# Memory attention in high and low parts, token-major values, and reordered evictions in a two-layer decoder trunk

## The chip, the cores and the metric

The kernel runs on one core of one Trainium2 chip. The metric is the device time of one execution in microseconds. Times in a profile are counted from the first instruction of the span.

## The reference

1024 tokens of width 1024 go through two layers. Each layer is: RMSNorm, one input projection, sparse attention (index scores, the 256 highest keys of a query, 8 heads) beside differential attention (4 heads), output projection and residual; RMSNorm and cross-attention into 256 memory tokens; RMSNorm and a gated MLP of width 2816 with a convolution of width 3. The part at which most of the change works:

```python
def _memory_attention(xn, memn, w_q, w_kv, w_o):
    b, s, _ = xn.shape
    m = memn.shape[1]
    q = (xn @ w_q).reshape(b, s, MEM_HEADS, MEM_HEAD_DIM)
    k, v = jnp.split(memn @ w_kv, 2, axis=-1)
    k = k.reshape(b, m, MEM_HEADS, MEM_HEAD_DIM)
    v = v.reshape(b, m, MEM_HEADS, MEM_HEAD_DIM)
    logits = jnp.einsum('bqhd,bkhd->bhqk', q, k,
                        preferred_element_type=jnp.float32) * MEM_HEAD_DIM ** -0.5
    p = jax.nn.softmax(logits, axis=-1)
    o = jnp.einsum('bhqk,bkhd->bqhd', p.astype(v.dtype), v).reshape(b, s, D_MODEL)
    return o @ w_o
```

There are 4 memory heads of 256 dimensions. The RMSNorm ahead of w_q is xn = h * rsqrt(mean(h*h)) * g, one factor per token.

## The kernel before, in words

**Data.** Activations lie feature-major: `xs_hi` and `xs_lo` are 8 chunks of 128 features by 1024 tokens. A float32 number is kept as a high part, rounded to fp32r by a copy, and a low part, the rest. A projection (`project`, L1933) adds three fp32r products for each 128-feature chunk: high weight by high x, high weight by low x, low weight by high x, each in two halves of 512 tokens.

**Weights.** `UNITS` lists 512 KB weight units in the order of use; two slots (`raw`, `w_hi`, `w_lo`) alternate. SyncE issues the load of a unit (L714) once the unit two before has its low part. ScalarE makes the high part (`split_hi`, L841) once the load has landed and TensorE is through with the unit two before. GpSimd makes the low part (`split_lo`, L780). Units "out", "km" and "vm" are split in two halves.

**PSUM.** There are 4 result buffers of 128x1024 ("banks" here). `JOBS` is the order of all results over time; job j uses bank j modulo 4, and TensorE waits in `claim` until job j-4 has been drained. Each engine's program is written out by hand in its own block, and an engine executes it strictly in that order.

**Start of a layer.** After projection unit 0 TensorE sums the squares for rows (`ssq`) and for columns (`ssq_columns`, L1974). ScalarE's `root_columns(0)` and then `root(0)` take Ln and Exp of each (L868, L870, L860, L862), VectorE makes `cos_t`, `sin_t` (L1401, L1402), the scales `qs`, `nqs` (L1404, L1405), clears masks (L1533, L1535), and only then rotates unit 0 and 1 (L1301 to L1310), which frees the bank that unit 2 needs.

**Index scores.** Behind unit `kb` 0 TensorE transposes the "va" tile (job TVW) and computes index scores of query blocks 7 and 6. ScalarE's loop over n first splits the weights of unit n+1, then evicts TVW (L1005, L1006) and the scores (`index_relus`, L977).

**End of sparse attention.** ScalarE copies the 8 chunks of `mixed` to `xs_hi` (L1064), VectorE makes `xs_lo` (L1674), and chunk by chunk ScalarE issues the load of the residual `h_t` over `mixed` (L1068), at most two in flight, waiting in its own queue. Behind these come the split of weight unit "out" 1 and the squares of the memory tokens (L1077), after which VectorE normalises them (L1689) and TensorE transposes them (TM0, L2118) between "out" 1 and "out" 2.

**Memory attention.** "km" and "vm" units project the memory tokens feature-major, 8 units of 128 columns each; `km_t` and `vmf` are copied from PSUM in float32 (L1100). Behind "qm" 0 TensorE sums the squares (L1960), then transposes `vmf` to token-major `vm` (TVM, L2131, evicted at L1106). VectorE multiplies each "qm" result by `rstd_q` (L1710). After all 8 "qm" units come scores SM (L2145), row maxima (L1717), Exp (L1118), normalisation (L1725), transposes TM (L2160, evicted by L1129) and the products with the values VM (L2169, evicted as high part at L1135 and low part at L1732), head after head, in float32: one float32 matmul shows as two matmul instructions in the trace.

**MLP.** "om" projections add to `h_t`; VectorE and ScalarE prepare sums of half-blocks X1, X3, X4, X6, X7 (`sum_blocks`, `high_blocks`, `low_blocks`), since gate and up projections use seven half-size products (`PRODUCTS`, L2194 to L2196) for each of 21 pairs f. Product i of pair f needs low weights (`product_lo`, L1788) and, from the fourth on, that VectorE or ScalarE has read an earlier result (`first_kept`, `second_read`, `c12_read`, `c21_read`). Blocks X7 are in `BLOCKS_THEN[2]` and serve product 6. After the last pair the "down" units read activations that come back from DRAM in chunks (`chunk_hi`, L1177, and `chunk_lo`, L1793).

## Time and profile before

| | |
|---|---|
| median of 3 runs | 3429.4 us (3424.77 to 3437.11) |
| the profiled execution | 3433.49 us, its span 3431.6 us |
| mean granted TensorE clock | 0.959 of full speed |
| TensorE matmul busy | 3118.2 us, 91% |
| VectorE busy | 2101.6 us, 61% |
| ScalarE busy | 1455.9 us, 42% |
| GpSimd busy | 827.0 us, 24% |
| DMA | 288.41 MB, mean 84 GB/s |

Busy time is the union of the instructions of an engine. The duration of one matmul in a row is its latency and overlaps the next; how fast matmuls go is read from the distance of their starts. An idle time stands in square brackets, with what ended it. Both layers are alike in the trace; layer 1 begins at about 1712 us.

### The profile page before, as it was taken

What the parts mean: (1) busy time and instruction counts of PE and PEld (TensorE: products, weight loads), DVE (VectorE), ACT (ScalarE), POOL (GpSimd) and SP (SyncE); (2) the same over time, 40 slices, a digit from 0 to 9 for tenths busy, and PEclk for the clock granted to TensorE, in tenths of its full rate; (3) what the DMA queues carried; (4) which work ended last, traced back from release to release, by engine and by line L of the source; (5) the groups of instructions that cost most, each with busy time, mean ns of one, the idle gap of its engine ahead of it and who ended that gap; (6) DMA issues with size and microseconds to landing.
All of it is one profiled execution on the core that took longest, in us unless ns stands there. A gap on an engine that the chain in (4) does not pass through costs nothing.

```text
span 3431.6 us, 39648 instructions
## 1 busy us (share of the span) xinstructions
PE 3118.2 (91%) x14848; PEld 2540.3 (74%) x14848; DVE 2101.6 (61%) x3615; ACT 1455.9 (42%) x2422; POOL 827.0 (24%) x422
## 2 busy tenths in 40 slices
PE   6897778889898999999998978879898999999998
PEld 4786765677587888878877867648785878887887
DVE  5488987340328989852447798752312598988324
ACT  5346867431325333321224677663313443334212
POOL 1111046351011222232211100644410212222321
PEclk8998999999999999999999989999999999999999
DMA  5454700331011222242242573012210222223322
GB/s 178 138 131 122 141 7 1 111 92 49 7 50 55 74 92 74 92 158 70 92 134 87 133 168 84 1 50 88 85 37 7 58 62 89 78 89 106 121 76 72
DMA packets 304046, 288.41 MB, mean 84 GB/s; under 512 B 19040, under 2 KB 266336, under 8 KB 303600
## 3 DMA queue, kind: packets, MB, share of 16 engines
q1 hardware_dynamic: 299456, 272.24, 28.0%
q10 hardware_dynamic: 4400, 13.63, 1.2%
q8 instruction: 119, 1.95, 0.2%
...
## 4 chain that ended last, share of the span: by engine, by line
PE 70%; DVE 16%; ACT 5%; DMA 4%; issue 3%; POOL 2%; SPq 1%; ACTq 0%; DVEq 0%; POOLq 0%
PE ps L1933 36%; PE ps L2194 8%; PE ps L2196 8%; PE ps L2195 7%; DVE junk L1436 3%; PE ps L2098 2%; PE ps L2169 2%; POOL w_lo L780 2%; DMA raw<-in_w_in 2%; PE ps L2145 2%; DVE p_a L1650 1%; DVE xbuf L1595 1%; PE ps L1987 1%; DVE xs_lo L1293 1%; PE ps L2090 1%
## 5 line engine op out<-in xcount | busy, mean ns | idle before, releaser
L780 POOL TENSOR_TENSOR w_lo<-raw,w_hi 128x512 fp32r<-128x512 f32 (+4 forms) x236 | 460.8, 1962 | 1503.9 <-ACT w_hi L841 1503.8
L1933 PE MATMUL ps<-xs_hi,w_hi 128*128 128x512 f32 (+1 forms) x1728 | 552.8, 402 | 73.1 <-POOL w_lo L780 29.5
L1933 PE MATMUL ps<-xs_lo,w_hi 128*128 128x512 f32 (+1 forms) x1728 | 544.5, 397 | 0.0
L1933 PE MATMUL ps<-xs_hi,w_lo 128*128 128x512 f32 (+1 forms) x1728 | 544.2, 397 | 0.0
L841 ACT ACTIVATE w_hi<-raw 128x512 fp32r<-128x512 f32 (+4 forms) x236 | 184.7, 803 | 737.0 <-PE ps L1933 585.1
L1680 DVE TENSOR_TENSOR h_t<-h_t,ps 128x1024 f32<-128x1024 f32 x96 | 117.3, 1221 | 568.0 <-PE ps L1933 568.0
L1933 PEld LDWEIGHTS ps<-xs_hi,w_hi 128*128 128x128 f32 (+1 forms) x1728 | 330.1, 193 | 154.8 <-issue 60.2
L1933 PEld LDWEIGHTS ps<-xs_lo,w_hi 128*128 128x128 f32 (+1 forms) x1728 | 331.4, 192 | 73.4
L1933 PEld LDWEIGHTS ps<-xs_hi,w_lo 128*128 128x128 f32 (+1 forms) x1728 | 330.1, 191 | 72.6
L803 POOL TENSOR_SCALAR p_a<-p_a,rca 128x1024 f32<-128x1024 f32 (+7 forms) x96 | 186.2, 1946 | 412.7 <-DVE rca L1623 411.5
L1172 ACT ACTIVATE w_hi<-w_sum 128x512 fp32r<-128x512 f32 x210 | 132.8, 633 | 323.7 <-DVE w_sum L1780 247.0
L2194 PE MATMUL ps<-xs_hi,w_hi 128*128 128x512 f32 x672 | 261.9, 390 | 7.4 <-issue 7.4
L2196 PE MATMUL ps<-xs_hi,w_lo 128*128 128x512 f32 x672 | 261.7, 389 | 0.0
L2195 PE MATMUL ps<-xs_lo,w_hi 128*128 128x512 f32 x672 | 261.7, 389 | 0.0
L1788 DVE TENSOR_TENSOR w_lo<-w_sum,w_hi 128x512 fp32r<-128x512 f32 x210 | 205.3, 978 | 16.7 <-ACT w_hi L1172 0.5
L2194 PE MATMUL ps<-act_hi,w_hi 128*128 128x512 f32 x504 | 196.8, 391 | 8.8 <-issue 8.8
L2196 PE MATMUL ps<-act_hi,w_lo 128*128 128x512 f32 x504 | 196.4, 390 | 0.0
L2195 PE MATMUL ps<-act_lo,w_hi 128*128 128x512 f32 x504 | 196.3, 390 | 0.0
L785 POOL TENSOR_TENSOR up<-up,rstd_f 128x512 f32<-128x512 f32 x42 | 73.6, 1752 | 450.8 <-DVE up L1869 450.8
L795 POOL TENSOR_TENSOR cv<-cv,up 128x1024 f32<-128x1024 f32 x44 | 106.3, 2417 | 203.4 <-ACT cv L1190 203.4
L2194 PEld LDWEIGHTS ps<-xs_hi,w_hi 128*128 128x128 f32 x672 | 126.2, 188 | 34.1 <-issue 8.2
L2196 PEld LDWEIGHTS ps<-xs_hi,w_lo 128*128 128x128 f32 x672 | 126.2, 188 | 26.2
...
## 6 DMA issues: line engine op xcount, KB each, us to landing
...
```

The costliest lines, as they stand in the source:

```text
L780: nc.gpsimd.tensor_tensor(w_lo[s][:, w], raw[s][:, w], w_hi[s][:, w].bitcast(f32), ALU.subtract).then_inc(lo_done, 1)
L795: nc.gpsimd.tensor_tensor(cv[:, f % 2, :], cv[:, f % 2, :], up[:, :], ALU.mult).then_inc(ga_done, 1)
L803: nc.gpsimd.tensor_scalar(p_a[:, g, i, 0:n], p_a[:, g, i, 0:n], rca[:, v % 2, i:i + 1], None, ALU.mult).then_inc(pa_pool, 1)
L841: A(w_hi[s][:, w], raw[s][:, w], ACT.Copy).then_inc(hi_done, 1)
L1172: A(product_weights(q)[0], weight_source(q), ACT.Copy).then_inc(phi_done, 1)
L1436: m = mark(V.tensor_scalar(junk[(nv - 1 - b) % 2][:, 0:w], keys(b), probe_v[:, b:b + 1], None, ALU.is_ge, ALU.add, accum_out=cnt_v[:, b:b ...
L1680: V.tensor_tensor(h_t[:, m, :], h_t[:, m, :], bank(job)[:, :], ALU.add).then_inc(drained_of(job), 1)
L1788: V.tensor_tensor(lo, weight_source(q), hi.bitcast(f32), ALU.subtract).then_inc(plo_done, 1)
L1933: ins = M(dst[0:c, a:b], w[s][:, k * c:(k + 1) * c], xt[:, a:b], start=(k == 0 and w is w_hi and part == 0), stop=(k == kc - 1 and w is w_lo))
L2194: M(dst, hi[:, wk], x_hi, start=(k == 0 and i < 3), stop=False, skip_group_check=True)
L2195: M(dst, hi[:, wk], x_lo, start=False, stop=False, skip_group_check=True)
L2196: ins = M(dst, lo[:, wk], x_hi, start=False, stop=(k == KC // 2 - 1), skip_group_check=True)
```

## The change

The parts, in the order of the program:

1. At the start of a layer `roots_in` takes both Ln first and both Exp after; `qs`, `nqs` and the masks come after the first rotation.
2. At the second unit of "kb" ScalarE splits the next weights after the index scores of block 7, not ahead of the TVW eviction.
3. `mixed` chunks 5, 6, 7 are copied to `xs_hi` ahead of the end of sparse attention; "out" 0 takes its chunks in the order 5, 6, 7, 4, 0, 1, 2, 3; the split of "out" 1 comes ahead of the loads of `h_t`.
4. "vm" units become 4 column groups of 256 by 2 halves of 512 features, with memory tokens stationary and weights moving (`project_memory_values`), so values come out token-major. The transposes TVM go.
5. Keys, queries, values and transposed probabilities are held as high and low fp32r parts; scores and value products are three fp32r matmuls in place of one float32. The per-token factor is applied in the scale of the Exp (`qs_m`) and of the maxima (`nqs_m`), and `ssq(1)` becomes `ssq_columns(1)`.
6. Scores and Exp of heads 0 and 1 stand among the "qm" units, by the list `MEMORY`.
7. In the MLP `product_lo(2)` and `(3)` come ahead of `taps(0)`; the X7 blocks are made one by one in the first four steps of pair 1; chunks 2 and 3 are made after the loop, so that the split of the first "down" unit no longer stands behind them.

```diff
-    memory = [("km", m, KC, P) for m in range(KC)] + [("vm", m, KC, P) for m in range(KC)]
+    memory = [("km", m, KC, P) for m in range(KC)] + [("vm", (p, h), KC // 2, 2 * P) for p in range(4) for h in range(2)]
...
+OUT_ORDER = [5, 6, 7, 4, 0, 1, 2, 3]
+MEMORY = [("qm", 0), ("ssqc", 1), ("qm", 1), ("qm", 2), ("SM", 0), ("qm", 3), ("qm", 4), ("SM", 1), ("qm", 5), ("qm", 6), ("qm", 7)]
+MEMORY += [("TM", 0), ("SM", 2), ("VM", 0), ("TM", 1), ("SM", 3), ("VM", 1), ("TM", 2), ("TM", 3), ("VM", 2), ("VM", 3)]
...
+            def roots_in():
+
+                rows, cols = ("ssq", 0), ("ssqc", 0)
+                wait_full(act, rows)
+                A(rstd_in[:, :], bank(rows)[:, :], ACT.Ln, scale=1.0 / D, bias=eps[:, 0:1]).then_inc(drained_of(rows), 1)
+                wait_full(act, cols)
+                A(rcol_l[:, :], bank(cols)[:, 0:NB], ACT.Ln, scale=1.0 / D, bias=eps[:, 0:1]).then_inc(drained_of(cols), 1)
+                wait_drained(act, rows)
+                A(rstd_in[:, :], rstd_in[:, :], ACT.Exp, scale=-0.5).then_inc(rstd_ready, 1)
+                wait_drained(act, cols)
+                A(rcol[:, :], rcol_l[:, :], ACT.Exp, scale=-0.5).then_inc(rcol_ready, 1)
+                act.wait_ge(rcol_ready, now["layer"] + 1)
...
-                    if n < N_PROJ:
+                    if n < N_PROJ and n != VW_AFTER + 1:
...
-                    seen = index_relus(I_BLOCKS.get(n - 1, []), seen)
+                    seen = index_relus(I_BLOCKS.get(n - 1, [])[:1], seen)
+                    if n == VW_AFTER + 1:
+                        split_hi(n + 1)
+                    seen = index_relus(I_BLOCKS.get(n - 1, [])[1:], seen)
...
+                        if (qb, g) == (1, 1):
+                            for k in OUT_ORDER[:3]:
+                                A(xs_hi[:, k, :], mixed[:, k, :], ACT.Copy).then_inc(xhi_done, 1)
...
+                for k in OUT_ORDER[3:]:
                     A(xs_hi[:, k, :], mixed[:, k, :], ACT.Copy).then_inc(xhi_done, 1)
-                for k in range(KC):
-                    after(act, xlo_done, KC + k + 1)
-                    after(act, back_dma[k % 2], 16 * (k // 2))
-                    act.dma_start(h_t[:, k, :], h_spill[k, :, :]).then_inc(back_dma[k % 2], 16)
-
-                for n in range(U_AT["out", 0], U_AT["vm", KC - 1] + 1):
-                    split_hi(n + 1)
+                split_hi(U_AT["out", 1])
+                for n, k in enumerate(OUT_ORDER):
+                    after(act, xlo_done, KC + n + 1)
+                    after(act, back_dma[n % 2], 16 * (n // 2))
+                    act.dma_start(h_t[:, k, :], h_spill[k, :, :]).then_inc(back_dma[n % 2], 16)
+
+                for n in range(U_AT["out", 0], KV_LAST + 1):
...
+                    if kind == "km":
+                        wait_full(act, ("unit", n))
+                        A(km_hi[:, m, :], bank(("unit", n))[:, 0:MEM], ACT.Copy).then_inc(kmhi_done, 1)
+                    elif kind == "vm" and half:
+                        wait_full(act, ("MV", p))
+                        A(vm_hi[:, :, 2 * P * p:2 * P * (p + 1)], memory_values(p), ACT.Copy).then_inc(vmhi_done, 1)
...
+                for kind, i in MEMORY:
+                    if kind == "qm":
+                        split_hi(U_AT["qm", i] + 1)
+                        wait_full(act, ("unit", U_AT["qm", i]))
+                        if i >= 4:
+                            wait_full(act, ("SM", (i - 4) // 2, 1))
+                        A(q_hi[:, i % 4, :], bank(("unit", U_AT["qm", i]))[:, :], ACT.Copy).then_inc(qmhi_done, 1)
+                    elif kind == "ssqc":
+                        root_columns(i)
+                    elif kind == "SM":
+                        mem_exps(i)
+                    elif kind == "TM":
+                        if i >= 2:
+                            wait_full(act, ("VM", i - 2, 1))
+                        for b in range(2):
+                            wait_full(act, ("TM", i, b))
+                            A(ptm(i, b)[0], bank(("TM", i, b))[:, :], ACT.Copy).then_inc(pthi_done, 1)
+                    else:
+                        for d in range(2):
+                            wait_full(act, ("VM", i, d))
+                            A(xs_hi[:, 2 * i + d, :], bank(("VM", i, d))[:, :], ACT.Copy).then_inc(xhi_done, 1)
...
+                        if f == 1 and i < len(BLOCKS_THEN[2]):
+                            high_blocks(BLOCKS_THEN[2][i:i + 1])
                         if i == 5:
                             if f == NF - 1:
                                 split_hi(DOWN)
                             gate_conv(f)
-                        if f == NF - 1 and i in (3, 4):
+                        if f == NF - 1 and i == 3:
                             wait_product(act, q)
-                            chunk_hi(2 * i - 6)
-                            chunk_hi(2 * i - 5)
+                            chunk_hi(0)
+                            chunk_hi(1)
+                chunk_hi(2)
+                chunk_hi(3)
...
+                wait_full(dve, a_transposes(*units[-1])[-1])
+                for n, k in enumerate(OUT_ORDER):
+                    after(dve, xhi_done, KC + n + 1)
                     V.tensor_tensor(xs_lo[:, k, :], mixed[:, k, :], xs_hi[:, k, :].bitcast(f32), ALU.subtract).then_inc(xlo_done, 1)
...
+                    for i in range(2 * (m - 2), 2 * (m - 1)) if 2 <= m < 6 else ():
+                        job = ("unit", U_AT["km", i])
+                        after(dve, kmhi_done, i + 1)
+                        V.tensor_tensor(km_lo[:, i, :], bank(job)[:, 0:MEM], km_hi[:, i, :].bitcast(f32), ALU.subtract).then_inc(drained_of(job), 1)
...
+                def value_lows(p):
+
+                    cols_p = slice(2 * P * p, 2 * P * (p + 1))
+                    after(dve, vmhi_done, p + 1)
+                    V.tensor_tensor(vm_lo[:, :, cols_p], memory_values(p), vm_hi[:, :, cols_p].bitcast(f32),
+                                    ALU.subtract).then_inc(drained_of(("MV", p)), 1)
...
+                def mem_normalise(h):
+
                     for c in range(2):
                         wait_drained(dve, ("SM", h, c))
                         link(V.reciprocal(rcm[:, c, :], smm[:, c, :]))
-                        V.tensor_tensor(pm[:, 4 * c:4 * c + 4, :], pm[:, 4 * c:4 * c + 4, :],
-                                        rcm[:, c, :].unsqueeze(2).to_broadcast([P, 4, MEM]), ALU.mult).then_inc(pm_ready, 1)
-                    if h < 3:
-                        mem_max(h + 1)
-                    for d in range(2):
-                        job = ("VM", h, d)
-                        after(dve, xhi_done, 3 * KC + 2 * h + d + 1)
-                        V.tensor_tensor(xs_lo[:, 2 * h + d, :], bank(job)[:, :], xs_hi[:, 2 * h + d, :].bitcast(f32),
-                                        ALU.subtract).then_inc(drained_of(job), 1)
+                        V.tensor_tensor(pm_at(h, c)[:, :, :], pm_at(h, c)[:, :, :], rcm[:, c, :].unsqueeze(2).to_broadcast([P, 4, MEM]),
+                                        ALU.mult).then_inc(pm_ready, 1)
+
+                for kind, i in MEMORY:
+                    if kind == "qm":
+                        job = ("unit", U_AT["qm", i])
+                        after(dve, qmhi_done, i + 1)
+                        V.tensor_tensor(q_lo[:, i % 4, :], bank(job)[:, :], q_hi[:, i % 4, :].bitcast(f32), ALU.subtract).then_inc(drained_of(job), 1)
+                        if i in (3, 5):
+                            mem_normalise(i // 2 - 1 if i == 3 else 1)
+                    elif kind == "ssqc":
+                        after(dve, rcolm_ready, 1)
+                        mark(V.tensor_scalar(qs_m[:, :], rcol_m[:, :], 1.0 / 16.0, None, ALU.mult))
+                        link(V.tensor_scalar(nqs_m[:, :], rcol_m[:, :], -1.0 / 16.0, None, ALU.mult))
+                    elif kind == "SM":
+                        mem_max(i)
+                    elif kind == "TM":
+                        for b in range(2):
+                            after(dve, pthi_done, 2 * i + b + 1)
+                            hi, lo = ptm(i, b)
+                            V.tensor_tensor(lo, bank(("TM", i, b))[:, :], hi.bitcast(f32), ALU.subtract).then_inc(drained_of(("TM", i, b)), 1)
+                    else:
+                        for d in range(2):
+                            job = ("VM", i, d)
+                            after(dve, xhi_done, 3 * KC + 2 * i + d + 1)
+                            V.tensor_tensor(xs_lo[:, 2 * i + d, :], bank(job)[:, :], xs_hi[:, 2 * i + d, :].bitcast(f32),
+                                            ALU.subtract).then_inc(drained_of(job), 1)
+                        if i < 2:
+                            mem_normalise(i + 2)
...
+                product_lo(2)
+                product_lo(3)
...
                         product_sum(q + 5)
+                        if f == 1 and i < len(BLOCKS_THEN[2]):
+                            sum_blocks(BLOCKS_THEN[2][i:i + 1])
+                            low_blocks(BLOCKS_THEN[2][i:i + 1])
+                        if f == NF - 1 and i == 3:
+                            chunk_lo(0)
+                            chunk_lo(1)
+                        if f == NF - 1 and i == 6:
+                            chunk_lo(2)
+                            chunk_lo(3)
                         if i == 6:
                             taps(f)
-                        if f == NF - 1 and i in (3, 4):
-                            chunk_lo(2 * i - 6)
-                            chunk_lo(2 * i - 5)
...
+            def project_memory_values(p, h):
+
+                n = U_AT["vm", (p, h)]
+                g = now["layer"] * U + n
+                s, c, kc = g % 2, UNITS[n][3], UNITS[n][2]
+                dst = claim(("MV", p)) if h == 0 else bank(("MV", p))
+                for b in range(2):
+                    to, t = dst[:, HALF * b:HALF * b + c], slice(b * P, (b + 1) * P)
+                    for i, ks in enumerate(parts(n)):
+                        pe.wait_ge(lo_done, splits(g, i))
+                        for k in ks:
+                            kk, w = h * kc + k, slice(k * c, (k + 1) * c)
+                            M(to, xm_hi[:, kk, t], w_hi[s][:, w], start=(h == 0 and k == 0), stop=False, skip_group_check=True)
+                            M(to, xm_hi[:, kk, t], w_lo[s][:, w], start=False, stop=False, skip_group_check=True)
+                            ins = M(to, xm_lo[:, kk, t], w_hi[s][:, w], start=False, stop=(h == 1 and k == kc - 1), skip_group_check=True)
+                ins.then_inc(vm_read if h == 0 else full_of(("MV", p)), 1)
...
+                                slot, k = (2 * h + d) % 4, 2 * h + d
+                                M(to, q_hi[:, slot, t], km_hi[:, k, :], start=(d == 0), stop=False)
+                                M(to, q_hi[:, slot, t], km_lo[:, k, :], start=False, stop=False)
+                                ins = M(to, q_lo[:, slot, t], km_hi[:, k, :], start=False, stop=(d == 1))
...
+                                hi, lo = ptm(i, b)
+                                for w, xs in ((vm_hi, (hi, lo)), (vm_lo, (hi,))):
+                                    for x in xs:
+                                        for a in (0, HALF):
+                                            ins = M(dst[:, a:a + HALF], w[:, b, v], x[:, a:a + HALF], start=(b == 0 and w is vm_hi and x is xs[0]),
+                                                    stop=(b == 1 and w is vm_lo))
```

## Rows read from the trace of the kernel before

**Rows 1.** Page, part 1: busy time, share of the span and instructions of each engine.

```profile
PE 3118.2 (91%) x14848; PEld 2540.3 (74%) x14848; DVE 2101.6 (61%) x3615; ACT 1455.9 (42%) x2422; POOL 827.0 (24%) x422
```

**Rows 2.** Stretches, in the columns of the first line: memory attention, then MLP pairs.

```profile
core 0: us, PE busy (x) PEld busy (x) DVE busy (x) ACT busy (x) POOL busy (x), PEclk, DMA share, GB/s
...
870.00:955.00 85.00, 70.93 (x263) 47.66 (x262) 31.27 (x40) 30.13 (x80) 0.00 (x0) 0.92 0.00 0
...
1092.00:1470.00 378.00, 378.00 (x1669) 313.30 (x1668) 341.27 (x417) 145.18 (x200) 83.63 (x40) 1.00 0.26 82
```

**Rows 3.** Chain that ended last, memory attention: start us, us, what.

```profile
870.75 13.81 PE ps L2145 x64
...
889.28 8.83 PE ps L2169 x16
...
947.77 6.87 PE ps L2169 x16
```

**Rows 4.** Chain and TensorE timeline: fp32r matmuls of 512 and of 256 columns.

```profile
129.91 10.94 PE ps L1933 x48
...
664.23 0.28 PE L1933 MATMUL ps<-xm_lo,w_hi 128*128 128x256 f32 x1
664.35 0.28 PE L1933 MATMUL ps<-xm_hi,w_lo 128*128 128x256 f32 x1
```

**Rows 5.** TensorE timeline: start, us, engine, line, what, count, idle before; behind "qm" 0.

```profile
784.84 1.88 PE L1960 MATMUL ps<-acc,ones 128*128 128x512 f32 x4
786.56 1.91 PE L2131 MATMUL ps<-ident_r,vmf 128*128 128x128 f32 x16
791.55 1.22 PE L1933 MATMUL ps<-xs_hi,w_hi 128*128 128x512 f32 x2 [3.08 <-DVE qm L1710]
792.57 1.06 PE L1933 MATMUL ps<-xs_lo,w_hi 128*128 128x512 f32 x2
...
797.56 0.63 PE L1933 MATMUL ps<-xs_lo,w_hi 128*128 128x512 f32 x2
```

**Rows 6.** Timeline of all engines at the starts of layers 0 and 1.

```profile
52.64 1.28 ACT L862 ACT_TABLE_LOAD   x1
...
65.30 1.92 DVE L1404 TENSOR_SCALAR qs<-rcol 128x8 f32<-128x8 f32 x1
...
70.41 1.22 PE L1933 MATMUL ps<-xs_hi,w_hi 128*128 128x512 f32 x2 [10.92 <-DVE y L1302]
...
1734.13 1.84 PE L1974 MATMUL ps<-ones,acc 128*128 128x1 f32 x16
...
1750.59 1.22 PE L1933 MATMUL ps<-xs_hi,w_hi 128*128 128x512 f32 x2 [3.51 <-DVE y L1302]
```

**Rows 7.** ScalarE and TensorE timelines at the first index scores.

```profile
120.39 1.06 ACT L841 ACTIVATE w_hi<-raw 128x1024 fp32r<-128x1024 f32 x1 [12.72 <-DMA raw<-in_w_in]
...
123.02 0.80 PE L1987 MATMUL ps<-k_idx,q_idx 128*128 128x512 f32 x1 [3.51 <-ACT wi L1006]
```

**Rows 8.** Chain, then TensorE and VectorE timelines, between "out" 0 and TM0.

```profile
626.87 4.51 DMA h_t<-h_spill
...
634.07 1.20 PE L1933 MATMUL ps<-xs_hi,w_hi 128*128 128x512 f32 x2 [4.59 <-POOL w_lo L780]
...
636.96 2.45 DVE L1689 TENSOR_SCALAR mem_tok<-mem_tok,rsm 128x1024 f32<-128x1024 f32 x2
```

**Rows 9.** Chain among the "vm" units.

```profile
746.86 4.04 DMA raw<-in_w_kv
...
751.70 4.05 POOL w_lo L780 x2
```

**Rows 10.** Timeline: the two evictions of a 128x1024 result.

```profile
898.15 1.02 ACT L1135 ACTIVATE xs_hi<-ps 128x1024 fp32r<-128x1024 f32 x1 [2.41 <-PE ps L2169]
899.20 1.23 DVE L1732 TENSOR_TENSOR xs_lo<-ps,xs_hi 128x1024 fp32r<-128x1024 f32 x1 [2.21 <-ACT xs_hi L1135]
```

**Rows 11.** TensorE timeline at product 2 of pair 1; chain ahead of "down".

```profile
1075.71 0.47 PE L2194 MATMUL ps<-xs_hi,w_hi 128*128 128x512 f32 x1 [3.70 <-issue]
...
1475.62 4.37 issue
```

245 lines of the change are left out of this document (112 added, 133 removed).

## The prediction

> **What bounds the kernel now.** I read the page first: TensorE is busy 91% of the span and the next engine, VectorE, 61% [rows 1]. So a gain must shorten TensorE's own work or one of its waits. Then I cut the span into stretches. The MLP pairs have no TensorE wait at all, though VectorE is busy 341 of 378 us there: nothing is to be had in them, and little room is left for new VectorE work. Memory attention is the stretch that looks worst: TensorE is busy 71 of 85 us, at a granted clock of 0.92 [rows 2]. The chain of waits names the work in it: float32 matmuls, 64 score instructions in 13.81 us (0.216 each) and 16 value instructions in 6.87 us (0.43 each); the same 16 took 8.83 us where they began slowly [rows 3]. Last I looked for waits of TensorE that come just before a stretch at half speed, since each costs twice. Behind "qm" 0 it waits 3.08 us for the scaled eviction, and the next pairs of matmuls start 0.86 us apart (1.2 GHz) until about 797; the usual distance of a pair is 0.456, from 48 matmuls in 10.94 us (2.4 GHz) [rows 4, 5]. Six pairs at that price are 2.5 us on top of the wait.
>
> **The change, part by part, per layer.**
>
> *Float32 to three fp32r products.* Scores: 4 heads x 32 instructions x 0.216 = 27.6 us go, 192 matmuls of 256 columns x 0.12 = 23.0 come (0.12 is the distance of two such starts) [rows 3, 4]. Values: 64 x 0.43 = 27.5 go, 96 x 0.228 = 21.9 come [rows 3, 4]. Gain 10.2 us.
>
> *Order of the heads.* From the start of the scores (870.6) to "om" 0 (954.6) are 84 us; matmuls of 27.6 + 27.5 and 64 transposes at 1.91 for 16 (7.6) [rows 3, 5] make 62.7, so 21.3 are waits and half clock. I drew up the new order with the durations of the two evictions, 1.02 on ScalarE and 1.23 on VectorE [rows 10]. Heads 0 and 1 have their scores and Exp under "qm" matmuls, 10.9 us each, with no wait. Behind "qm" 7 the transposes of head 0 and the scores of head 2 cover the evictions, and so on; per head TensorE has 5.75 + 1.9 + 5.5 = 13.1 us, VectorE some 10.5 (two maxima, two normalisations, four low parts), ScalarE some 8. Only once does TensorE run dry: VectorE normalises head 3 after both low parts of VM 1, about 4 us after TM 2 has ended. With 2 us of half clock behind it that leaves 6 of the 21.3. Gain 15.3 us; bounds 5 (a 2.5 us wait with its half clock in each head remains) and 21.
>
> *Behind "qm" 0.* TVM (1.91), the wait (3.08) and the half clock (2.5) go. The row sum (4 instructions, 1.7 us net) becomes the column sum, 1.84 us [rows 5, 6]: nothing. The multiplication by the root leaves the path; what is late next is the bank of "qm" 1, long free. Gain 7.5 us. VectorE's eight scalings become eight subtractions, and ScalarE gains eight copies, under 10.9 us each.
>
> *"vm" units.* Same bytes, same matmul count. Their pace is a loop of load 4.04, high part about 0.65 (half an eviction [rows 10]), two low parts 4.05, for every two units, 4.45 per unit against 2.9 us of matmuls [rows 9]. The new loads have lines of 1 KB in place of 512 B. No row shows this size alone; a load cannot get cheaper than half (2 us) and I bound it by no gain. I take 1 us off each, so 0.45 per unit for some 6 units: 2.5 us, bounds 0 and 5. The profile shows 512 B lines moving 512 KB in 4.04 us [rows 9]. The Trainium skill, DMA: Bandwidth & Descriptors, Specifications, puts line rate at 512 B and up; by it this term would be 0.
>
> *Start of the layer.* Two table loads of 1.28 go from ScalarE's chain and the row sum need not wait for the column sum: the roots come 3.9 us sooner. `qs` and the masks leave the path of the rotation: 2.7 us in layer 0, where the stalled `qs` (1.92) is seen, 1.0 in layer 1. TensorE's wait was 10.92 and 3.51 [rows 6]. So 6.5 us in layer 0; in layer 1 the whole wait and 2.6 of half clock, 6.1. What is late next: VectorE's second product in layer 0, TensorE itself in layer 1. Moved `qs` and masks hide behind unit 2. In the profile ScalarE loads a table (1.28) for the Exp that directly follows a Ln [rows 6]. The Trainium skill, ScalarE: Activation LUTs, Table sets: the hidden batching unit, has one set with both; by it the merge would save no load and this term would be 2.6 less. The trace speaks against that rule here.
>
> *Index scores.* ScalarE's split waits for a load until 120.39 and TensorE waits 3.51 us behind it [rows 7]. After the change the TVW eviction goes first. The wait is replaced by a short one: "kb" 1 needs the bank of the first score of block 6, whose eviction now stands behind the split (126.4 in my count, against 129.9). Gain 3.5 us; queued behind the split is only that eviction.
>
> *"out" 0 to TM0.* The 4.59 us wait before "out" 1 [rows 8] goes, because its split is ahead of the loads of `h_t`. But those loads start at about 624 instead of 617 and still go at 4.51 us a pair [rows 8], so ScalarE is free at about 637.8. Squares, root and VectorE's normalisation (2.45 for two [rows 8]) end TM0's wait at about 643 to 644, where "out" 1 has ended at 638. Most of the gain turns into a wait at TM0. The three early copies of `mixed` also delay the last transposes by 3 us and take away a 3.6 us wait for the first low part. Net 1.3 us; bounds 0 and 6.
>
> *MLP, start.* The 3.70 us wait for product 2 [rows 11] shrinks to 0.8. But X7 blocks made one by one cost a round trip between ScalarE and VectorE each (about 2 us against 1.3 in a batch, from halved evictions [rows 10]), and they now stand ahead of `second_read`, `c12_read` and `c21_read`, for which products 4 to 6 wait. In my count product 6 ends 1.2 us later than before. Loss 1.5 us; bounds a loss of 4 and a gain of 3.
>
> *MLP, end.* The split of "down" 0 no longer stands behind chunks 2 and 3, and the wait of 4.37 us [rows 11] goes. Chunk 3 is ready at about 1478.7, needed at 1479.4. Gain 4.4 us.
>
> **Sum.** Layer 0: 10.2 + 15.3 + 7.5 + 2.5 + 6.5 + 3.5 + 1.3 - 1.5 + 4.4 = 49.7; layer 1 49.3. Together 99 us off the profiled execution of 3433.5, so 3334.5. That execution is 4.1 us above the median; against the median of 3429.4 the forecast is about 3331.
>
> **Rivals.**
>
> *Evictions bound memory attention.* Each result now needs two evictions instead of one, and each head's chain alternates between engines. For: VectorE already ends most waits around softmax, and 10.5 of 13.1 us leaves little room. Against: the order leaves each eviction a job of TensorE as cover. Price: 5 us per head, 40 in all: 3371.
>
> *The early gains are swallowed.* Between 260 and 480 us VectorE's search sets the end; if it is paced by something that does not move, start and index gains and "out" (some 22 us) are lost: 3353. Against: the search begins with the scores, which move.
>
> *More than I count.* The loads of `h_t` go faster together, and the MLP start gains: 6 + 3 us more per layer and the upper bounds of "vm" and of the heads: 3308.
>
> *Slower: half clock throughout memory attention.* The clock falls behind short waits and transposes: pairs at 0.86 where 0.456 is usual [rows 5]. If the many small jobs with a wait each kept TensorE at 1.2 GHz for the whole new stage, its 52.5 us of matmuls would take 105, in both layers 105 more: 3436, which is 7 above before. It decides from the point where over 94% of the stage is at the lower level. Against: the old stage, with worse waits, had 0.92 [rows 2]. The Trainium skill, TensorE: Matmul & The Clock Gate, A second HAM failure mode: psum-queue depth-cycling, describes such a loss from micro-idles between groups.
>
> *It does not do what it says.* The three products might not run at 0.12 and 0.228 where each stationary tile is used once for 256 columns. The projections of the memory tokens do just that at 0.12 [rows 4], so this gets little.
>
> **How the numbers follow.** Forecast as summed 0.57; evictions bound 0.15; early gains swallowed 0.12; more than I count 0.11; slower 0.03; products not at their pace (3350) 0.02. A measurement of this kernel tells about 0.3% (10 us) from no change. All cases but the slower one are over 50 us below, so faster gets 0.96; half of the slower case's chance falls within 10 us. The range, 3304 to 3372, takes in the bounds of the heads, "vm", "out" and MLP start, and both middle rivals.
>
> **What would show it.** Right: no TVM and no scaling between "qm" 0 and 1, starts of "qm" 1 directly behind the column sum; 59 us from the first score to "om" 0 less the "qm" work, with one wait of about 4 us ahead of TM 3; a new wait ahead of TM0 on the normalised memory tokens; waits before products 4 and 5 of pair 1; none ahead of "down". Wrong: waits of TensorE for low parts in each head, a granted clock below 0.9 in memory attention, or index and start gains that are gone by 480 us.

## The result, and the profile after the change

The kernel after takes 3330.6 us (median of 4 runs, 3329.3 to 3333.5) where the kernel before, timed beside it, takes 3429.6: ratio 0.9717, 95% interval 0.9701 to 0.9732. Forecast was 3331. The profiled execution has a span of 3327.8 us against 3431.6, with the engines busy as follows (page, part 1; before: [rows 1]):

```profile
PE 3067.8 (92%) x15032; PEld 2534.5 (76%) x15032; DVE 2146.4 (64%) x3659; ACT 1464.1 (44%) x2422; POOL 828.7 (25%) x422
```

A total tells little about nine terms, so I cut both traces at the same events of TensorE: the first column sum of a layer, the last index score, the first and last score of the sparse attention (`k_a`), the first key matmul of the memory tokens, "qm" 0, "om" 0, the first "gate" matmul that waits for `xs_lo`. These are rows of TensorE's timeline of the kernel after (start us, us, engine, line, what, count, idle before), with the waits that matter between them:

```profile
44.59 1.84 PE L2094 MATMUL ps<-ones,acc 128*128 128x1 f32 x16
...
61.98 1.17 PE L2036 MATMUL ps<-xs_hi,w_hi 128*128 128x512 f32 x2 [4.39 <-DVE y L1358]
...
154.81 0.52 PE L2108 MATMUL ps<-k_idx,q_idx 128*128 128x384 f32 x1
...
595.36 0.28 PE L2108 MATMUL ps<-k_a,q_a 128*128 128x128 f32 x1
...
641.33 0.28 PE L2036 MATMUL ps<-xm_hi,w_hi 128*128 128x256 f32 x1
...
755.29 0.70 PE L2036 MATMUL ps<-xs_hi,w_hi 128*128 128x512 f32 x2 [0.93 <-issue]
...
766.29 1.84 PE L2094 MATMUL ps<-ones,acc 128*128 128x1 f32 x16
767.99 0.72 PE L2036 MATMUL ps<-xs_hi,w_hi 128*128 128x512 f32 x2
...
888.32 3.48 PE L2273 MATMUL ps<-ident_r,pm_odd 128*128 128x128 f32 x16 [4.60 <-DVE pm_odd L1802]
...
902.57 0.61 PE L2036 MATMUL ps<-xs_hi,w_hi 128*128 128x512 f32 x2
...
1000.04 0.73 PE L2036 MATMUL ps<-xs_hi,w_hi 128*128 128x512 f32 x2 [0.76 <-DVE xs_lo L1349]
...
1031.19 0.55 PE L2315 MATMUL ps<-act_hi,w_hi 128*128 128x512 f32 x1 [4.77 <-issue]
1031.53 0.63 PE L2316 MATMUL ps<-act_lo,w_hi 128*128 128x512 f32 x1
1031.96 0.63 PE L2317 MATMUL ps<-act_hi,w_lo 128*128 128x512 f32 x1
...
1039.08 0.77 PE L2315 MATMUL ps<-act_hi,w_hi 128*128 128x512 f32 x1 [3.32 <-issue]
...
1044.34 0.63 PE L2315 MATMUL ps<-xs_hi,w_hi 128*128 128x512 f32 x1
```

The stretches between such starts, layer 0 / layer 1, and what the prediction's terms add up to in each:

| stretch | before | after | gain | predicted |
|---|---|---|---|---|
| layer start to last index score | 122.3 / 117.5 | 110.2 / 105.0 | 12.1 / 12.5 | 10.0 / 9.6 |
| to first sparse score | 289.8 / 290.6 | 289.3 / 289.2 | 0.4 / 1.4 | 0 |
| to last sparse score | 148.6 / 151.0 | 151.2 / 149.1 | -2.6 / 1.9 | 0 |
| to first memory key matmul | 51.8 / 51.5 | 46.0 / 47.2 | 5.9 / 4.3 | 1.3 |
| to "qm" 0 | 113.1 / 113.5 | 114.0 / 113.4 | -0.8 / 0.1 | 2.5 |
| to "om" 0 | 181.9 / 181.9 | 147.3 / 148.4 | 34.6 / 33.5 | 33.0 |
| to the first "gate" wait | 97.9 / 97.9 | 97.5 / 97.5 | 0.4 / 0.5 | 0 |
| MLP, to the next layer or the end | 682.2 / 676.6 | 683.9 / 678.8 | -1.8 / -2.2 | 2.9 |

The rows sum to 48.2 and 52.0 us; another 1.9 us lie ahead of the first column sum. So memory attention came out to within 2 us, and it is two thirds of the gain. Beside it, start, index and "out" gave more than I had counted, "vm" and the MLP less than nothing. The new memory attention, as stretches (before: the 85 us at 0.92 of [rows 2]):

```profile
core 0: us, PE busy (x) PEld busy (x) DVE busy (x) ACT busy (x) POOL busy (x), PEclk, DMA share, GB/s
755.00:853.00 98.00, 97.71 (x484) 83.14 (x485) 24.24 (x26) 27.10 (x51) 19.34 (x9) 1.00 0.17 49
853.00:903.00 50.00, 45.40 (x272) 40.64 (x271) 29.56 (x32) 24.72 (x49) 0.00 (x0) 0.97 0.00 1
```

TensorE is never idle under the query tiles and idle once among the heads, for the 4.60 us above; the row behind it, 16 transposes in 3.48 us where the usual is 1.91 [rows 5], is the lower clock that follows the wait (granted 0.57 from 888.32 to 892).

### The profile page after: what moved, and what is told of

It is laid out like the page before. It is cut to its first block, busy times and chain, and to the rows that moved or that the text cites. A ratio compares the mean times of both kernels' runs of the same rounds, so it can differ in the third digit from the quotient of the medians.

```text
span 3327.8 us, 40059 instructions
## 1 busy us (share of the span) xinstructions
PE 3067.8 (92%) x15032; PEld 2534.5 (76%) x15032; DVE 2146.4 (64%) x3659; ACT 1464.1 (44%) x2422; POOL 828.7 (25%) x422
## 4 chain that ended last, share of the span: by engine, by line
PE 71%; DVE 15%; ACT 5%; issue 3%; DMA 3%; POOL 2%; SPq 0%; ACTq 0%; DVEq 0%; POOLq 0%
PE ps L2036 37%; PE ps L2315 8%; PE ps L2316 8%; PE ps L2317 8%; DVE junk L1501 3%; PE ps L2218 2%; POOL w_lo L805 2%; DVE p_a L1715 1%; DMA raw<-in_w_in 1%; DVE xbuf L1660 1%; DVE xs_lo L1349 1%; PE ps L2210 1%; PE ps L2289 1%; DMA h_t<-h_spill 1%; PE ps L2107 1%
## 5 line engine op out<-in xcount | busy, mean ns | idle before, releaser
L2036 PE MATMUL ps<-xs_hi,w_hi 128*128 128x512 f32 (+1 forms) x1728 | 541.4, 395 | 36.1 <-POOL w_lo L805 23.7
L2036 PE MATMUL ps<-xs_lo,w_hi 128*128 128x512 f32 (+1 forms) x1728 | 537.3, 392 | 0.0
L2036 PE MATMUL ps<-xs_hi,w_lo 128*128 128x512 f32 (+1 forms) x1728 | 536.1, 392 | 0.0
L1746 DVE TENSOR_TENSOR h_t<-h_t,ps 128x1024 f32<-128x1024 f32 x96 | 117.1, 1220 | 517.7 <-PE ps L2036 502.8
L2036 PEld LDWEIGHTS ps<-xs_hi,w_hi 128*128 128x128 f32 (+1 forms) x1728 | 322.5, 189 | 115.6 <-issue 35.6
L1886 DVE TENSOR_TENSOR w_lo<-w_sum,w_hi 128x512 fp32r<-128x512 f32 x210 | 201.5, 960 | 16.8 <-ACT w_hi L1225 1.4
```

The costliest lines, as they stand in the source:

```text
L1746: V.tensor_tensor(h_t[:, m, :], h_t[:, m, :], bank(job)[:, :], ALU.add).then_inc(drained_of(job), 1)
L1886: V.tensor_tensor(lo, weight_source(q), hi.bitcast(f32), ALU.subtract).then_inc(plo_done, 1)
L2036: ins = M(dst[0:c, a:b], w[s][:, k * c:(k + 1) * c], xt[:, a:b], start=(at == 0 and w is w_hi and part == 0), stop=(at == kc - 1 and w is ...
```

## The experiments

All are edits to the kernel after, whose 3330.6 us they are to be held against; each was timed beside the kernel before. The edits are shown shortened and partly in words. The stretches of the same untouched code differ by 1 to 3 us between executions, one of them by more (last section), so I read an edit first in its own stretch and then in the time.

**1. Order without the arithmetic.**

```diff
-M(to, q_hi[:, slot, t], km_hi[:, k, :], ...); M(to, q_hi.., km_lo..); M(to, q_lo.., km_hi..)
+M(to, q_hi[:, slot, t].bitcast(f32), km_hi[:, k, :].bitcast(f32), ...)      # the value products likewise
```

> The order of the kernel after, with its evictions in high and low parts, but every product of the memory attention's scores and values made once in fp32 on the high parts, as many columns as before the change (the two low products of each are left out, so the output lacks them). My theory is that the arithmetic is a term of its own of 10.2 us a layer, from the paces of the two kernels (three fp32r products of 256 columns 0.36 us against 0.43 for one in fp32, of 512 columns 0.68 against 0.86), and that the order gives the rest: the stretch from query tile 0 to output tile 0 goes from 147.4 to about 157 us (a little less than 10.2, since a longer product of head 1's values covers part of the wait of 4.6 us ahead of head 3's transposes), the time to 3349. The rival 'evictions set the pace': longer products only fill waits, stretch 147 to 149, time 3331 to 3335. The rival 'the arithmetic was nearly all of the gain of 35 us': stretch 170 or more, time 3376 or more.

Measured: 3350.0 us; the stretch 155.6 / 156.0 us. So arithmetic is 8.4 / 7.6 of the 34.6 / 33.5 us, order and the cut behind "qm" 0 are 26.2 / 25.9. The wait ahead of head 3 shrank, as expected, which hides a part of the pace. TensorE's timeline of this kernel:

```profile
755.96 0.70 PE L2036 MATMUL ps<-xs_hi,w_hi 128*128 128x512 f32 x2 [1.82 <-issue]
...
895.15 3.26 PE L2271 MATMUL ps<-ident_r,pm_odd 128*128 128x128 f32 x16 [3.41 <-DVE pm_odd L1802]
...
911.59 1.03 PE L2036 MATMUL ps<-xs_hi,w_hi 128*128 128x512 f32 x2
```

**2. One product for three.**

```diff
-M(to, q_hi.., km_lo..); M(to, q_lo.., km_hi..); values: for w, xs in ((vm_hi, (hi, lo)), (vm_lo, (hi,)))
+                                                 values: vm_hi by hi alone
```

> The kernel after with one fp32r product (high by high) in place of three in the memory attention's scores and values; the low products are left out, the evictions stay. It takes 128 products of 0.12 us and 64 of 0.227 us a layer off the matrix engine, 29.9 us. If the matrix engine were the bound throughout, the stretch from query tile 0 to output tile 0 falls from 147.4 to 117.5 and the time to 3271. If the evictions set the pace everywhere, nothing changes (3331). My theory is in between: up to the last query tile the matrix engine is the bound (7.7 us come back there), and among the heads Vector has 16 low parts of 1.14 us, 4 maxima of 1.25 and 4 scalings of 1.35 in what would be 28 us, so that waits take some 10 us back: stretch about 128, time about 3291.

Measured: 3298.4 us; the stretch 131.8 / 131.7, so 15.5 / 16.8 of the 29.9 us are gained. As far as the last query tile TensorE stays busy throughout; the 7.7 us there are gained whole. Among the heads (first transpose to "om" 0, layer 0) 22 us of products went and only 7.8 are gained, 46.7 to 38.9 us. TensorE's idle time there grew from 4.6 to 13.2 us, and the granted clock fell from 0.96 to 0.82. Its four largest waits, in total, times, longest (`q_lo` of L1822 is the buffer of the low transposed probabilities):

```profile
PE ps L2271 <- DVE pm_odd L1802: 5.0, 1, 5.0
PE ps L2285 <- DVE q_lo L1822: 3.0, 2, 2.7
PE ps L2271 <- ACT pm_even L1163: 2.5, 2, 2.1
PE ps L2271 <- ACT pm_odd L1163: 2.0, 2, 1.1
```

**3 and 4. The seventh product's blocks.**

```diff
-product_lo(2); product_lo(3); taps(0); up; ...  for i in loop: sum_blocks(X7[i]); low_blocks(X7[i])
+taps(0); up; product_lo(2); product_lo(3); sum_blocks(X7); low_blocks(X7); loop         # 3: as before, ScalarE's high_blocks likewise
```

> The kernel after with the four blocks of the seventh product sum made as before: all four in one go ahead of the loop over the products, the low parts of weights 2 and 3 behind the scaled first 'up' tile. My theory is that the making of one block in each product is what costs at the start of the MLP: Vector then has 3.95 us of work and waiting in each of four products of 2.72 us, 0.79 us of it idle behind Scalar's high part. Undone, the two waits of 4.77 and 3.32 us go, one of about 3.7 us ahead of product 2 comes back, and the seventh product starts 2.9 us earlier in each layer: time 3325. The rival is that the start is late for the clock's sake (0.89 in that stretch) or for other work of Vector and that the order of the blocks gives nothing: 3331.

```diff
 if f == 1 and i < 4: sum_blocks(X7[i:i + 1])
-if f == 1 and i < 4: low_blocks(X7[i:i + 1])
+if f == 1 and 0 < i <= 4: low_blocks(X7[i - 1:i])                                       # 4
```

> The kernel after with each block's low part made one product later than its sum and high part, so that Vector does not wait for Scalar's high part in between. If the round trip of 0.79 us in each of four products is the cost, the chain of Vector is 3.2 us shorter by the fourth product, the seventh product starts about 3 us earlier in each layer, and the time is 3325. If it is the work itself (3.16 us in each product against 2.72 us of matrix work), or the clock, what comes back is under 1 us a layer: 3329 to 3331.

Measured, 3: 3324.7 us. The seventh product starts 39.95 us behind the "gate" wait of layer 0, where the kernel after needs 44.30 (1044.34 less 1000.04) and the kernel before 39.96; in layer 1 it is 42.1 against 44.2 after and 39.9 before. TensorE's timeline of the third run:

```profile
1004.86 0.73 PE L2034 MATMUL ps<-xs_hi,w_hi 128*128 128x512 f32 x2 [0.77 <-DVE xs_lo L1348]
...
1028.61 0.77 PE L2313 MATMUL ps<-xs_hi,w_hi 128*128 128x512 f32 x1 [3.70 <-issue]
...
1042.00 0.47 PE L2313 MATMUL ps<-act_hi,w_hi 128*128 128x512 f32 x1 [2.34 <-issue]
...
1044.81 0.39 PE L2313 MATMUL ps<-xs_hi,w_hi 128*128 128x512 f32 x1
```

The old wait of 3.70 is back [rows 11] and still the product comes sooner, in part because TensorE waits less: 4.77 + 3.32 + 0.60 us of waits cost more than 3.70 + 2.34. Run 4, which keeps the early product 2 and takes only the round trip away, starts it at 39.9 / 42.2 us: the same. By its time (3330.2, four runs from 3322.6 to 3341.1) it says nothing. What the round trip is, VectorE's timeline of the kernel after shows, one block of four:

```profile
1032.21 0.68 DVE L1850 TENSOR_TENSOR xs_raw<-h_t 128x512 f32<-128x512 f32 x1
1033.68 0.75 DVE L1863 SCALAR_TENSOR_TENSOR xs_lo<-xs_raw,packs,xs_hi 128x512 fp32r<-128x512 f32 x1 [0.79 <-ACT xs_hi L1210]
1034.35 0.68 DVE L1953 TENSOR_TENSOR kept<-ps,kept 128x512 f32<-128x512 f32 x1
...
1036.16 0.68 DVE L1850 TENSOR_TENSOR xs_raw<-h_t 128x512 f32<-128x512 f32 x1
```

A block's period is 3.95 us, in which a product of 12 matmuls takes 2.72, and `kept`, which the next products need, stands behind the block.

**5 and 6. Index weights and layer start.**

```diff
-if n < N_PROJ and n != VW_AFTER + 1: split_hi(n + 1)      # behind the first index block
+if n < N_PROJ: split_hi(n + 1)                            # 5: as before
-roots_in(); ... if n == 2: query_scales(); first_masks()
+root_columns(0); root(0); query_scales(); ... first_masks() ahead of the units    # 6
```

> The kernel after with the high part of the unit behind the index weights made ahead of the index scores' first block, as before the change. My theory (the term of 3.5 us a layer): the wait for the index weights on Scalar comes back behind a load, the second key tile starts 3.5 to 4.6 us later in both layers, time 3338 to 3340. The rival, that the early weights were hidden by what follows (key tiles that wait for something else), gives 3331.

> The kernel after with the start of a layer as before: the column sum's root first and then the row sum's, the query scales and the first masks ahead of the first unit. My theory: the whole start term comes back, 6.5 us in layer 0 and 6.1 in layer 1 (less 1.7 us in layer 0 that the sum of squares gave by its clock alone, which stays), time 3341 to 3343. The rival, that Exp and Ln would need no change of table and the roots' order is worth nothing, leaves only the wait for the query scales: 2.6 us a layer less, 3336 to 3338.

Measured, 5: 3341.6 us, start to last index score 117.3 / 112.2 (after: 110.2 / 105.0), so 7.1 / 7.2 and not 3.5. ScalarE's and TensorE's timelines of this run:

```profile
114.50 1.06 ACT L866 ACTIVATE w_hi<-raw 128x1024 fp32r<-128x1024 f32 x1 [14.08 <-DMA raw<-in_w_in]
...
117.12 0.80 PE L2105 MATMUL ps<-k_idx,q_idx 128*128 128x512 f32 x1 [4.86 <-ACT wi L1046]
```

Counted from the first column sum, TensorE reaches the index scores 6.5 us sooner than in the kernel before (66.5 in place of 73.0), but the load that ScalarE waits for lands only 5.1 us sooner (68.8 in place of 73.9). So ScalarE waits 14.08 us for it and TensorE 4.86, against 12.72 and 3.51 in [rows 7]. 6: 3340.3 us, the same stretch 117.1 / 110.7, so 6.8 / 5.8; TensorE's waits of 10.90 and 3.50 are back [rows 6].

The kernel before has neither part, so the four kernels also price each part by itself: run 6 (new index order, old start) is 5.3 / 6.8 us under the kernel before, run 5 (new start, old index order) 5.0 / 5.3. Both together give 12.1 / 12.5. Each part is worth more beside the other, and the two undone prices, 13.9 / 13.0, count what they share twice. But the index part is over 3.5 even on the old start. One reason is that the index scores behind the wait run at a lower granted clock: 0.62 in this row of the kernel before (columns as in the rows of the new memory attention above, the clock third from the end), 1.00 in run 6 over the same microseconds:

```profile
123.00:130.00 7.00, 6.98 (x22) 5.94 (x23) 6.65 (x6) 4.81 (x6) 0.95 (x1) 0.62 0.65 232
```

**7. "out" as before.**

```diff
-OUT_ORDER = [5, 6, 7, 4, 0, 1, 2, 3]
+OUT_ORDER = [0, 1, 2, 3, 4, 5, 6, 7]      # no early copies; split_hi("out" 1) behind the loads
```

> The kernel after with the output projection's first unit over the chunks in order 0 to 7, all eight high copies behind the last head, and the second unit's high part behind the loads of the residual. My theory: the section from the last head to output tile 2 got 3.3 us shorter in layer 0 and about 4.6 in layer 1 by the change, more than the 1.3 I had predicted, and all of it by this part: time 3337 to 3340. The rival, that the early copies only moved the wait (the tail waits for Vector's rows 3 us more) and that the gain there comes from the clock: 3331 to 3333.

Measured: 3342.9 us; last sparse score to first memory key matmul 53.5 / 51.8 us, against 46.0 / 47.2 after and 51.8 / 51.5 before. All of the gain there is this part's. TensorE's timeline of run 7 has the old waits [rows 8] again, each with a slow first pair behind it:

```profile
604.86 1.19 PE L2031 MATMUL ps<-xs_hi,w_hi 128*128 128x512 f32 x2 [3.68 <-DVE xs_lo L1735]
...
622.06 1.19 PE L2031 MATMUL ps<-xs_hi,w_hi 128*128 128x512 f32 x2 [4.74 <-POOL w_lo L805]
```

In the kernel after both are gone, and in their place stand a later tail and short waits at TM0:

```profile
600.85 1.09 PE L2210 MATMUL ps<-ident_r,p_a 128*128 128x128 f32 x4 [5.21 <-DVE p_a L1694]
...
627.83 1.06 PE L2240 MATMUL ps<-ident_r,mem_tok 128*128 128x128 f32 x8 [1.13 <-DVE mem_tok L1755]
```

ScalarE's queue says why TM0's wait is short. The first loads of `h_t` go out at 605.94, 10.6 us behind the last sparse score, where the kernel before has 9.6 (616.80 less 607.25); only the third stands behind the new split, at 611.86. In ScalarE's program all of them stand behind five copies and the split; the queue issued the first two while those copies were still being made (605.68 to 610.5, split at 610.44). In layer 1 TM0's waits are 2.46 and 0.61.

**8. VectorE beside GpSimd.**

```diff
-gained_low(l, G_MQ, 2 * KC, k)
+gained_low(l, G_MQ, 2 * KC, k, P)         # 128 of 1024 columns
```

> The kernel after with Vector's eight low parts of the gained residual among the memory's value units made on 128 of 1024 columns (the rest left out, so the query tiles lack them). In the kernel after GpSimd's low weights take 2.0 us each there, and 1.27 where Vector is idle, and the matrix engine waits for them. My theory: Vector beside GpSimd is what the value units are slow by; GpSimd's low parts fall to about 1.3 us, the units' loads come earlier, and the stretch from the first value unit to query tile 0 gets 3 to 5 us shorter a layer (of this up to 1 for the chain of the low parts itself): time 3321 to 3325. The rival: the loads of 512 KB set the pace (5.18 us one by one), GpSimd is faster and waits longer for them: under 1.5 us a layer, 3328 to 3331.

Measured: 3324.3 us; first memory key matmul to "qm" 0 109.8 / 110.2 us against 114.0 / 113.4. Groups of GpSimd in the value units, in the kernel after and in this run (shapes, count, busy us and mean ns, idle before):

```profile
L805 POOL TENSOR_TENSOR w_lo<-raw,w_hi 128x512 fp32r<-128x512 f32 x14 | 26.5, 1919 | 11.7 <-ACT w_hi L866 11.7
```

```profile
L805 POOL TENSOR_TENSOR w_lo<-raw,w_hi 128x512 fp32r<-128x512 f32 x14 | 19.7, 1432 | 14.1 <-ACT w_hi L866 14.1
```

GpSimd's low part goes from 1.92 to 1.43 us for no edit of its own, and the loads of the "vm" units are issued as little as 3.3 us apart where it was 4.45.

**9. MLP end as before.**

```diff
-i == 3: chunk_hi(0), chunk_hi(1); behind the loop: chunk_hi(2), chunk_hi(3); chunk_lo(2), (3) at i == 6
+i in (3, 4): chunk_hi(2 * i - 6), chunk_hi(2 * i - 5); chunk_lo likewise, behind taps
```

> The kernel after with the high and low parts of the MLP's chunks 2 and 3 made as before, with product 4 of the last tile rather than behind product 6. My term was a gain of 4.4 us a layer (the wait of 4.37 ahead of the first 'down' unit); with the start of the MLP now priced at 4.3 to the bad by the third run, the MLP as a whole leaves only some 2.6 for this part, since in the kernel after the low parts of chunks 2 and 3 (two in 4.41 us beside GpSimd) and late low weights hold the matrix engine for 0.25, 0.57 and 1.32 us. So undone: the stretch from the first gate unit to the next layer's sum 2.6 us longer, time 3336. Had the term been whole, 3339; were the end not worth anything, 3331.

Measured: 3339.7 us; the MLP's stretch 685.9 / 681.5 us, 1.9 / 2.8 more than in the kernel after, with a wait of 4.00 ahead of "down" 0. The stretch says what I expected; the time says 9 us, of which the stretches of this edit hold 4.7. The rest lies in stretches that it does not touch.

**10 and 12. VectorE's scalings earlier and later.**

```diff
+if i == 1: mem_normalise(3)               # 10: ahead of VM 1's low parts
 for d in range(2): ... xs_lo[:, 2 * i + d] ...
-if i < 2: mem_normalise(i + 2)
+if i == 0: mem_normalise(2)
```

> The kernel after with Vector's scaling of head 3's probabilities ahead of the low parts of head 1's values rather than behind them. In the kernel after Vector idles 4.19 us there while Scalar makes head 3's exponentials ahead of the evictions that Vector waits for, then makes two low parts (2.36) and only then the scalings, and the matrix engine waits 4.60 us ahead of head 3's transposes, which then run at half clock. My theory: it is this order in Vector's queue, not Vector's or Scalar's load, that makes the wait; it goes, and the stretch from query tile 0 to output tile 0 falls from 147.3 and 148.4 to about 143: time 3321. The rival, that the wait only moves on to head 2's values (whose low parts come 2.7 us later), leaves 1 to 2 us a layer: 3327 to 3329.

```diff
-if i in (3, 5): mem_normalise(...)        # heads 0 and 1, among the query tiles
+if i == KC - 1: mem_normalise(0); mem_normalise(1)      # 12
```

> The kernel after with Vector's scalings of the probabilities of heads 0 and 1 behind the last query tile's low part, rather than among the query tiles: the one piece of the heads' order that can be moved back by itself. My theory: the order's gain (26 of the 35 us a layer by the first run) comes from Vector and Scalar doing the heads' first steps under the query tiles, where Vector idles 5 to 9.7 us a tile; moved out of that cover, the transposes of head 0 start behind 858.35 plus two times 1.34 us rather than at 855.86, 5.2 us later, and at a lower clock, which adds 1 to 1.7: stretch from query tile 0 to output tile 0 153 to 155 in place of 147.3 and 148.4, time 3341 to 3344. The rival, that the wait ahead of head 3 (4.60 us) takes it up, or that the scalings are hidden wherever they stand: stretch 148 to 150, time 3331 to 3334.

Measured, 10: the stretch 142.8 / 142.9 us, as expected. VectorE's timeline shows its idle time used, TensorE's the wait gone:

```profile
882.42 1.22 DVE L1802 TENSOR_TENSOR pm_odd<-pm_odd,rca 128x1024 f32<-128x1024 f32 x1
...
884.61 1.22 DVE L1802 TENSOR_TENSOR pm_odd<-pm_odd,rca 128x1024 f32<-128x1024 f32 x1
885.75 2.35 DVE L1829 TENSOR_TENSOR xs_lo<-ps,xs_hi 128x1024 fp32r<-128x1024 f32 x2
...
887.03 2.22 PE L2275 MATMUL ps<-ident_r,pm_odd 128*128 128x128 f32 x16 [1.12 <-DVE xs_lo L1829]
```

The 1.12 us that are left wait for VM 1's low part, whose bank head 3's transposes need. The time, 3328.3 (3326.7 to 3332.0), is only 2.3 us under the kernel after where the two stretches are 10.0 shorter; in the profiled execution 3.6 of that went in layer 1's stretch from the last index score to the first sparse score. Why all four executions show it I cannot say. 12 (head 0's probabilities are divided by head 1's sums in it, since the sums have one buffer): 3354.0 us, the stretch 153.9 / 155.6, a new wait of 5.16 ahead of head 0's transposes, which then take 3.28 us, and the 4.61 ahead of head 3 as before. Nothing took the wait up. The time is 10 us over my 3344, 7.8 of them in the profiled execution in layer 1's stretch ahead of the sparse scores, again.

**11. Three mended.**

```diff
 run 3 + run 10 +
-if n == DOWN + 1: gate_up(NF - 1)
+if n == DOWN + 2: gate_up(NF - 1)         # GpSimd: third "down" unit's low part first
```

> Three edits to the kernel after together: the blocks of the seventh product sum as before the change (third run, 6.3 us by the stretches), Vector's scaling of head 3 early (9 to 10 us by theory), and GpSimd's low part of the third 'down' unit ahead of the last tile's gating, which holds it 1.32 us back in each layer (2 to 2.6 us). If the three are independent: 3331 less 6.3, 9.5 and 2.3, about 3313. If the scaling's wait only moves on, 3320 to 3322; if the parts overlap or the clock takes some back, in between.

Measured: 3313.8 us (3310.6 to 3319.7), ratio to the kernel before 0.9667 (0.9651 to 0.9683), as summed. Against run 3 (3324.7) the early scaling and GpSimd's order together give 10.9, so the scaling's 10 us are there in this company. The wait of 1.32 in "down" is gone from TensorE's timeline, the two of 0.25 and 0.57 stand.

## Why the prediction was right

**Float32 to fp32r (10.2 us):** right; run 1 shows 8.4 / 7.6 with a shorter wait (3.41 for 4.60) behind it, so 9.6 / 8.8 for the pace against 10.2.

**Order of the heads (15.3) and behind "qm" 0 (7.5):** right. Together 26 us against 22.8 [run 1]. The traces part the stretch further. From the end of "qm" 0 to "qm" 1 it is 6.71 us before and 1.70 after, and "qm" 1 to 7 lose 2.5 us of lower clock: 7.5 us in both layers, as forecast. "qm" 0 itself takes 11.0 us in place of 12.6, since it began at a granted clock of 0.66 before (772 to 777), which no term held. The heads are left with 25.5 / 24.3 us for arithmetic and order together, forecast 25.5. "qm" 1 starts directly behind the column sum (766.29 and 767.99), TensorE waits once, 4.60 us, for the very instruction that I had named. Run 12 shows that cover is worth that much: two scalings moved from under the query tiles to behind them cost 6.6 / 7.2 us. The rest of the order (some 10 us a layer) was not undone by itself; that it too comes from cover is argued from the single wait, not shown.

**The rival "evictions bound memory attention"** does not hold for this kernel, but run 2 shows how near it is: of 22 us of matmuls taken from among the heads 14 were not gained: 8.6 of them became waits for both evicting engines, the other 5.8 are matmuls that take longer at the lower clock. The rivals of half clock and of swallowed early gains fell with the trace: clock 1.00 and 0.97 in memory attention, and the early gains pass through both stretches of the search (-2.6 to 1.9). "More than I count" was added up wrongly: 6 + 3 us a layer, 2.5 for "vm" and 5.7 for the heads make 34 in both layers, so 3297 and not 3308, outside the range. In the "vm" term 0.45 for 6 units is 2.7.

**Layer start (6.5 / 6.1):** right, 6.8 / 5.8 by run 6 (5.0 / 5.3 on the old index order), 10.92 to 4.39 by the wait. In the kernel after ScalarE loads one table (1.28 us at 46.75) between the two Ln and the two Exp, where the roots before had three; over the whole kernel 25 loads against 29. No run changes the loads alone. So the trace stays against the Trainium skill's rule that one set holds both (ScalarE: Activation LUTs, Table sets: the hidden batching unit).

**Index (3.5): mis-sized.** It measured 7.1 / 7.2 undone, 5.3 / 6.8 on the old start and, start and index together, 12.1 / 12.5 for my 10.0 / 9.6. The step that failed is "Gain 3.5 us": it prices layer 0's wait and nothing behind it. The scores behind the wait ran at 0.62 of the clock for 7 us, which is 2.7 us; layer 1's wait is 4.78 and not 3.51; and with the new start the wait would have grown to 4.86 / 5.81, since the load does not come sooner by all that the start does.

**"out" (1.3; bounds 0 and 6): mis-sized,** 5.9 / 4.3. The step that failed is "those loads start at about 624 instead of 617": I had the split ahead of all loads of `h_t`, but the early copies have their low parts ready, and two loads leave ahead of it. TM0's waits, some 5 us in my count, are 1.13 and 0.61, and the lower clock behind the two old waits, which I had not counted, goes too: of the 5.9 us 3.4 are waits, and the granted clock of the stretch is 0.93 in place of 0.90.

**"vm" (2.5; bounds 0 and 5): wrong,** -0.8 / 0.1, a little below the lower bound. Two steps failed. "I take 1 us off each" load: they did get shorter, but by 0.46. The issues of these loads in layer 1, before and then after (size, median us from issue to landing):

```profile
raw<-in_w_kv SPq DMA_DIRECT2D x8, 512.0 KB, 3.9
raw<-in_w_kv SPq DMA_DIRECT2D x8, 512.0 KB, 3.5
```

Over both layers the medians are 3.96 and 3.50 us, and 3.45 to 3.58 in all twelve runs, though two or three of the 16 take over 4.5 (5.18 on the chain of the kernel after). The "km" loads, whose lines are as before, stay at 3.98 and 3.92. And "so 0.45 per unit": a shorter load does not shorten the loop, because GpSimd fills it. In layer 1 the loads are issued 4.45 us apart in both kernels; before, GpSimd waited 0.2 to 0.4 us for each unit's high part, after, it makes ten low parts without a gap. Before, then after:

```profile
2433.19 4.05 POOL L780 TENSOR_TENSOR w_lo<-raw,w_hi 128x512 fp32r<-128x512 f32 x2 [0.39 <-ACT w_hi L841]
...
2354.43 21.31 POOL L805 TENSOR_TENSOR w_lo<-raw,w_hi 128x512 fp32r<-128x512 f32 x10 [7.35 <-ACT w_hi L866]
```

Run 8 shows what sets GpSimd's pace: VectorE's low parts beside it. Its part takes 1.92 us, and a quarter less as soon as VectorE has less to do. The Trainium skill's rule (DMA: Bandwidth & Descriptors, Specifications: full rate from 512 B), by which the term is 0, gave the stretch better than I did, but not the load, which is 0.46 us shorter with lines of 1 KB. That it is the line size no run shows by itself, since none changes it alone.

**MLP start (-1.5; bounds -4 and +3): wrong size,** -4.3 in both layers, just outside the bounds. The step "in my count product 6 ends 1.2 us later" counts waits and the round trip (0.79 us a block by the trace, four times 3.2), and nothing for the clock. From the "gate" wait to the seventh product TensorE waits 8.69 / 9.73 us after and 8.11 / 8.04 before, so only 0.6 / 1.7 more. The granted clock of the stretch is 0.89 / 0.92 after and 1.00 before, and the same matmuls take 3.8 / 2.6 us more: behind the wait of 4.77 they start 0.43 us apart in place of 0.228 (1031.53 and 1031.96). Runs 3 and 4 take 2.2 to 3.0 us off the waits of either layer, about the four round trips; both start the seventh product at 39.9 us in layer 0, and at 42.1 and 42.2 in layer 1, at a granted clock that stays at 0.89 to 0.92. Why it falls, no run shows. A wait alone is not enough: the kernel before and run 3 wait 3.70 us for the same product, and behind the wait one is granted the full clock and the other half of it (before, then run 3):

```profile
1075.71:1078.60 2.89, 2.89 (x12) 2.14 (x12) 2.89 (x6) 1.75 (x3) 0.00 (x0) 1.00 0.00 0
...
1028.61:1034.00 5.39, 5.39 (x13) 4.23 (x14) 5.39 (x9) 4.24 (x7) 0.00 (x0) 0.50 0.00 0
```

**MLP end (4.4): mis-sized,** 1.9 / 2.8 by run 9. In place of the wait of 4.37 (3.66 in layer 1) stand three of 0.25, 0.57 and 1.32 us. "Chunk 3 is ready at about 1478.7, needed at 1479.4" did not hold: VectorE's two low parts take 4.41 us, where the kernel before has 2.37 for the same pair, and GpSimd works beside them for some 3 us. The 1.32 is GpSimd's late third "down" unit, which I had at nothing and which run 11 removes. The rows of the kernel after:

```profile
1428.37 0.70 PE L2036 MATMUL ps<-xs_hi,w_hi 128*128 128x512 f32 x2
...
1431.62 0.73 PE L2036 MATMUL ps<-xs_hi,w_hi 128*128 128x512 f32 x2 [0.25 <-DVE xs_lo L1891]
...
1433.85 0.73 PE L2036 MATMUL ps<-xs_hi,w_hi 128*128 128x512 f32 x2 [0.57 <-DVE xs_lo L1891]
...
1442.25 0.70 PE L2036 MATMUL ps<-xs_hi,w_hi 128*128 128x512 f32 x2 [1.32 <-POOL w_lo L805]
```

```profile
1429.39 4.41 DVE L1891 TENSOR_TENSOR xs_lo<-xs_raw,xs_hi 128x1024 fp32r<-128x1024 f32 x2 [0.27 <-ACT xs_hi L1230]
```

That GpSimd is what slows the pair is read from the rows; no run takes GpSimd's work away there.

So against 99 us stand 102.2 up to the start of the last matmul (3414.7 and 3312.5), with start, index and "out" some 6 us a layer better than forecast and "vm" and the MLP some 8 worse. The largest terms were right by themselves; that five wrong ones cancel, and the median with them lands within 1 us of the forecast, is luck.
